# A single-core decoder layer: who turns the state-space output, and in which order ScalarE ends that stage

## The reference, cut to what matters

```python
y = jax.nn.gelu(y.reshape(bsz, seq, S5_WIDTH))
y = y * jax.nn.sigmoid(y @ w_glu + b_glu)
...
gates = jax.nn.sigmoid(gate_logits.reshape(bsz, seq, N_BRANCHES, D_MODEL))
projected = jnp.einsum('bsnw,nwd->bsnd', branches, w_branch)
merged = jnp.einsum('bsnd,bsnd->bsd', gates, projected)
```

## Time and profile before

| what | value |
|---|---|
| median of 3 runs (lowest, highest) | 1408.01 us (1407.98, 1408.33) |
| the profiled execution's own time | 1408.35 us |
| its span, first to last instruction | 1406.6 us |
| PE busy | 1396.8 us, 99% of the span |
| VectorE, ScalarE, GpSimd busy | 74%, 49%, 12% |
| mean granted TensorE clock | 1.00 |

### The profile page before, as it was taken

How to read it: one execution, slowest core, us unless ns; L and a number is a source line. 1 busy time by engine, 2 the same in 40 slices (tenths; PEclk the granted TensorE clock), 3 DMA queues, 4 the chain that set the end, 5 groups by cost and what they waited for, 6 DMA issues and landing times.

```text
span 1406.6 us, 19078 instructions
## 1 busy us (share of the span) xinstructions
PE 1396.8 (99%) x6986; PEld 1166.7 (83%) x6986; DVE 1038.2 (74%) x1527; ACT 684.6 (49%) x1111; POOL 165.4 (12%) x174
## 2 busy tenths in 40 slices
PE   9999999999999999999999999999999999999999
PEld 7988888888788888878888888888888888888887
DVE  6888666656876657769545888778877777588886
ACT  6344356656555431266323755555555555434332
POOL 2002511103361021123000100000000000000000
PEclk9999999999999999999999999999999999999999
DMA  7022211241121223277622222222222224890222
GB/s 266 30 84 69 76 53 61 66 136 38 55 61 40 83 76 91 77 247 253 239 92 75 60 90 90 72 78 90 90 75 90 87 64 147 316 386 4 97 75 82
DMA packets 131111, 149.99 MB, mean 107 GB/s; under 512 B 11402, under 2 KB 93245, under 8 KB 130621
## 3 DMA queue, kind: packets, MB, share of 16 engines
q1 hardware_dynamic: 130832, 148.72, 32.1%
q10 hardware_dynamic: 189, 0.08, 0.0%
HBM read 111.88 MB, written 36.31 MB: 105 GB/s over the span
## 4 chain that ended last, share of the span: by engine, by line
PE 97%; DVE 1%; ACT 1%; DMA 1%; issue 0%; SPq 0%; POOL 0%; ACTq 0%
PE ps L2566 30%; PE ps L945 18%; PE ps L2875 5%; PE ps L2876 5%; PE ps L2877 5%; PE ps L2966 4%; PE ps L1152 3%; PE ps L3528 2%; PE ps L3530 2%; PE ps L3529 2%; PE ps L1129 2%; PE ps L482 2%; PE ps L484 2%; PE ps L483 2%; PE ps L1848 2%; PE ps L443 1%
## 5 line engine op out<-in xcount | busy, mean ns | idle before, releaser
L2566 PE MATMUL ps<-split_arena 128*128 128x512 f32 x1320 | 306.4, 389 | 0.8 <-ACT up_part L2451 0.8
L2566 PEld LDWEIGHTS ps<-split_arena 128*128 128x128 f32 x1320 | 247.6, 188 | 52.6 <-issue 1.2
L945 PE MATMUL ps<-split_arena 128*128 128x512 f32 x1152 | 290.3, 399 | 0.5 <-ACT plain_arena L980 0.4
L945 PEld LDWEIGHTS ps<-split_arena 128*128 128x128 f32 x1152 | 208.6, 188 | 41.5 <-issue 1.5
L2749 ACT ACTIVATE down_ops<-down_all 128x1024 fp32r<-128x1024 f32 x77 | 81.5, 1061 | 114.9 <-PE ps L2877 112.9
L2768 DVE TENSOR_TENSOR down_ops<-down_all,down_ops 128x1024 fp32r<-128x1024 f32 x77 | 94.0, 1221 | 45.7 <-ACT down_ops L2749 45.6
L2566 PE MATMUL ps<-up_b,split_arena 128*128 128x512 f32 x528 | 127.0, 389 | 0.0
L2875 PE MATMUL ps<-down_ops 128*128 128x512 f32 x308 | 119.9, 389 | 0.0
L2876 PE MATMUL ps<-down_ops 128*128 128x512 f32 x308 | 119.8, 389 | 0.0
L2877 PE MATMUL ps<-down_ops 128*128 128x512 f32 x308 | 119.8, 389 | 0.0
L2566 PEld LDWEIGHTS ps<-up_b,split_arena 128*128 128x128 f32 x528 | 99.0, 188 | 20.5
(11 more groups left out here) (452 smaller groups left out, 2598.3 us busy)
## 6 DMA issues: line engine op xcount, KB each, us to landing
plain_arena<-in_w_in SPq DMA_DIRECT2D x26, 512.0 KB, 4.0
scr_gate<-plain_arena SPq DMA_DIRECT2D x48, 256.0 KB, 2.0
plain_arena<-scr_gate SPq DMA_DIRECT2D x24, 512.0 KB, 4.5
plain_arena<-in_w_up SPq DMA_DIRECT2D x22, 512.0 KB, 5.2
up_raw<-in_w_up SPq DMA_DIRECT2D x22, 512.0 KB, 4.8
scr_act<-plain_arena SPq DMA_DIRECT2D x22, 512.0 KB, 2.6
down_all<-scr_act SPq DMA_DIRECT2D x18, 512.0 KB, 9.7
down_all<-in_w_down SPq DMA_DIRECT2D x18, 512.0 KB, 10.8
```

Source lines behind the costliest of these rows:

```text
L945: mm = nc.tensor.matmul(m.ps[:, self.banks[half], :], w[:, k, :], src[:, k, h * BANK:(h + 1) * BANK], start=(j == 0), stop=(j == self.PER_ ...
L2566: mm = nc.tensor.matmul(o, self.w[j][w][:, k, :], self.h[j][k][h], start=(j in self.OPENS and k == 0 and n == 0), stop=(k == self.HK - 1 a ...
```

## The change

ScalarE makes two of the four copies of turned y (quarters 1 and 3), VectorE keeps quarters 0 and 2. ScalarE's list becomes: Gelu; a wait for the last filling matmul; the split of the first branch weights; the two copies of turned y; the copy of the last gate half; the other two splits; the rest as it was. The first two branch weight loads move on SP ahead of the next-to-last gate store; the third stays where it was.

```diff
+    def copy_turned(f, copy, eng):
+        mt, half = divmod(f, 2)
+        eng.wait_ge(s["yt_ps"], 2 * mt + 2)
+        copy(y_t[:, mt, HALF_ROWS[half], :].rearrange("p c s -> p s c"),
+             ps[:, 4 + f, :].rearrange("p (s c) -> p s c", s=CH)).then_inc(s["yt_cp"], 1)
...
-    def sync(sp, between):
+    def sync(sp, early, between):
...
         sp.dma_start(w_glu, m.ins["s5_w_glu"][0].rearrange("(k p) n -> p k n", p=P)).then_inc(s["glu_in"], 16)
+        early(sp)
         fill.store(sp, 0)
         sp.wait_ge(s["y_ps"], 4)
         between(sp)
...
-    def scalar(act):
+    def scalar(act, first_split):
...
         fill.scalar(act, S5_LAST)
+        act.wait_ge(fill.half_mm, 2 * fill.count)
+        first_split(act)
+        for f in (1, 3):
+            copy_turned(f, lambda to, src: A(to, src, ACT.Copy), act)
         fill.copy_made(act)
...
-        for f in range(4):
-            mt, half = divmod(f, 2)
-            dve.wait_ge(s["yt_ps"], 2 * mt + 2)
-            V.tensor_copy(y_t[:, mt, HALF_ROWS[half], :].rearrange("p c s -> p s c"),
-                          ps[:, 4 + f, :].rearrange("p (s c) -> p s c", s=CH)).then_inc(s["yt_cp"], 1)
+        for f in (0, 2):
+            copy_turned(f, V.tensor_copy, dve)
...
-            branch.sync(sp, lambda sp: [load_raw(sp, 0, u) for u in range(READY)])
+            branch.sync(sp, lambda sp: [load_raw(sp, 0, u) for u in range(2)], lambda sp: load_raw(sp, 0, 2))
...
-            branch.scalar(act)
-            for u in range(READY):
+            branch.scalar(act, lambda act: split(act, 0, 0))
+            for u in range(1, READY):
                 split(act, 0, u)
```

## The result

The changed kernel took 1410.24 us, the median of 20 executions (1409.17 to 1411.31), against 1408.14 (1407.78 to 1408.54) of 20 of the kernel before beside it: 2.1 slower, ratio 1.0016, 95% interval [1.001, 1.0022]. The forecast was 1409.2 with a range to 1410.1: the sign was right, the size not, and the time lies above the range. The distance from the lowest to the highest execution grew too, from 0.8 to 2.1.

A forecast was written before the change was run, and what follows sets the result against it. PE, busy 99% of the span, bounds the kernel, so only its holes can move. Hole loss 1.37 less GLU gain 0.14 gives 1.23 on the 1408.01 median: 1409.2 us, range 1407.8 to 1410.1.

The forecast's parts named there:

- The hole before the first projection: PE's idle after its transposes: projection starts at 606.03 instead of 604.66, behind ScalarE's queued gate-half copy; loss 1.37.
- The copied-out condition: Before the first projection PE needs all 48 gate halves copied out; met at 603.40 before, forecast to be late next.
- The copy's price: ScalarE's scattered copy of turned y: 0.596 plain plus VectorE's scatter cost 0.466, taken as 1.06 each.
- The GLU's gain: VectorE's two fewer copies let the GLU matmuls start right after the first projection: gain 0.14, between 0 and 0.42.
- no table load: On ScalarE: the change adds no table load; the only one here, 1.28 before the first sigmoid, stays covered.
- no sharing between the two engines: Against the rival that ScalarE and VectorE share one pace for scattered writes: loss 3.49, time 1411.5, chance 0.03.
- The gate loads come later, "Cost 0": SP's last store and gate loads come 2.58 later; the wait of 0.15 before the third projection stays, cost 0.
- the slack of 0.27: GLU tail: ScalarE free at 615.8, 0.27 ahead of the last sigmoid at 616.07; gates later than that cost one for one.
- a rival with 0.43: Gates late: at the median landing of 4.5 the GLU tail is 0.43 later, time 1409.7; late-gates chance 0.10.
- The clock: Rival: after the longer hole the granted clock halves for the first projection's 12 matmuls, adding 2.87; time 1412.1, chance 0.03.
- What can be told apart: Whole kernel: a measurement can tell about 0.2%, 2.8 us, from no change; chance of a result within it 0.91.

The follow-up runs named there:

- experiment 1: Changed kernel with ScalarE's copy of the last gate half put ahead of its two copies of turned y: 1407.83 us against 1408.09 before, ratio 0.9998.
- experiment 7: Changed kernel with ScalarE's two copies written in one run of 512 instead of every eighth element: 1408.94 us, ratio 1.0007 to the kernel before.
- experiment 10: The kernel before, unchanged, run again for a second profile of its gate loads: 1407.96 us.
- 6: Changed kernel with first four gate loads issued ahead of the last gate store, repeated: five executions 1408.92 to 1409.45 us, five 1410.42 to 1411.05.
- 14: The changed kernel, unchanged, run again with eight executions for a third profile: 1410.64 us (1409.74 to 1410.93).
- 2: Changed kernel with the first four gate loads issued ahead of the last gate half's store: 1410.31 us, ratio 1.0014, in two groups of times.
- experiment 8: Changed kernel with all three first branch weight loads back where they were before: 1409.95 us, ratio 1.0014 to the kernel before.
- experiment 13: The changed kernel, unchanged, run again with eight executions for a second profile: 1410.54 us (1409.52 to 1410.80).
- early-gates kernel: Changed kernel with the first four gate loads issued ahead of the last gate half's store, run twice: first median 1410.31 us, ratio 1.0014.
- experiment 9: Changed kernel with eight matmuls of no use in PE's 2.06 hole ahead of the first projection: 1409.84 us, ratio 1.0013 to the kernel before.

## Why the prediction was wrong in size

- *The hole before the first projection* (loss forecast 1.37, in the profile 1.32): right, with its mechanism. The copied-out condition took the place of the weights, ScalarE's line 980 ended the wait, and experiment 1 took it away.
- *The copy's price* (1.06 from VectorE's scatter, measured 1.11 and 1.14): right in kind, 0.07 short. ScalarE also began the second copy earlier, 0.88 after the first and not 0.95, so the end came where I had put it. That the hole came out within 0.05 is in part luck: two small errors cancel. Here the Trainium skill (SBUF — State Buffer, section Door 1: The DMA port swizzle), with its penalty for accesses that each enter a new 16-byte line, fits ScalarE as well. The per-element price without a term for stride in the Trainium skill (ScalarE: Activation LUTs, section What ACT_TABLE_LOAD costs) holds only for the plain copy of experiment 7.
- *The GLU's gain* (0.14, measured 0.15), *no table load*, *no sharing between the two engines*: right. With VectorE's copies beside them ScalarE's plain copies took 0.60.
- *The gate loads come later, "Cost 0"*: this step failed. It cost 0.88 in the profile. Two things were wrong in it. The first is the landing: the forecast took the second gate's from the one profile, 4.9 after its issue; it was 5.83 in the profile after and 5.2 to 5.8 elsewhere. The second is the slack of 0.27, which was found by following ScalarE alone to the GLU's last sigmoid. ScalarE did keep that pace: free 4.0 after the gate's sigmoid by the forecast, it began the last GLU sigmoid 4.09 after it. But the chain after shows VectorE as the engine that is late, with products and low parts back to back from 615.62 to 618.13. By the 7.07 of the table, the forecast's own sigmoid at 611.80 leads to a third projection at 618.87, and PE was forecast there at 617.70 + 1.23 = 618.93: the slack was 0.06. The sigmoid in fact began at 612.50 + 0.18 = 612.68, 0.88 behind the forecast, and 0.88 - 0.06 = 0.82 is what the third projection came late by, 619.57 + 0.18 = 619.75. The text carried the rule, "one for one if the gates land more than 0.27 later", and a rival with 0.43, but gave it a tenth. It had priced that rival from the first gate's 3.8 and the median of 4.5 over all loads of line 2928; the second gate is the one that decides, and the median of the four loads at this place was 5.3 in the same profile and 5.9 in experiment 10.
- *The clock*: taken for a rival at 3 in 100, and this failed too. It fell in two of the six profiles with the 2.06 hole (experiments 6 and 14; not in 2, 8, 13 and the profile after), and by the mean clock of each execution in 36 of 68: 21 of 36 of the changed kernel, 4 of 11 in experiment 8, 11 of 21 of the early-gates kernel. Price: 1.6, not the 2.87 I had. At the lower level the matmuls start 0.43 apart in place of 0.23, nearly the doubling that I took, but that level lasted 3.4 and not for all twelve. Behind a late gate only 0.6 to 1.2 of the 1.6 is left. Its share in the changed kernel's median is 0.2 to 0.4 (experiment 9), and it is the source of the times above 1410.3. The warning on idle gaps that I quoted from the Trainium skill (TensorE: Matmul & The Clock Gate, section Why this matters for your kernels) agrees in kind with what these traces show behind the hole of 2.06; that this trace had held 1.00 through a hole of 0.74 said nothing of one of 2.06.
- *What can be told apart*: I took 2.8 us as the least that shows. With 20 executions of each the interval, 1.001 to 1.0022, leaves out 1 at 2.1 us.

Sum by the runs: 1.32 - 0.15 + 0.88 = 2.05 in the profiled execution at full clock, whose own time is 2.1 above the median before. It had the latest landing of the six, 5.83; experiment 13's profile, with 5.25, took 1409.57, 1.5 above before. The ten executions of the changed kernel without a fall have their median 1.9 above before, and the clock brings the median of all 20 to 2.1. At 1410.01 those ten would have been just inside the range: the late gates took the time to its end, and the clock over it.

Not tried: whether a later order of the two output weight loads would bring the second gate in sooner. Nor do the runs show why one landing takes 4.9 and another 5.8, or why the clock falls in one execution and not in the next.

## What to carry to other kernels

An engine that works in order and has slack is no place for extra work ahead of the one small instruction that others wait for: put the released resource's copy first, then the new work (experiment 1 against the change, 2.4 us apart by medians). When a change delays the issue of a load, take the scatter of its landing from several profiles before calling the slack enough, and follow the work behind it through every engine up to the wait, not through one. And look at holes in a busy TensorE twice: the hole's length, and what the granted clock does behind it.

## What the runs showed of the hardware

ScalarE pays for writes that go to every eighth float as VectorE does: 1.11 to 1.14 for 128x512 against 0.60 for the same copy in one run. A hole of 2.06 in TensorE, behind 32 small transposes, was followed by a mean clock under 1.00 in 36 of 68 executions; in the two profiles that caught it the clock was at its lower level for some 3.4, and TensorE's work took 1.6 longer. With a hole of 1.20, or with eight 128x512 matmuls inside the hole of 2.06, none of 11 executions each showed it. The second of four gate loads, behind the same store, landed between 4.9 and 5.8 after its issue.
